# A hybrid block and a two-layer block on one core: the second block's weight halves written by transfers

## What is computed

```
h = concat(meta_tokens, x)                         # 528 x 1024
h = h + diff_attention(rms_norm(h), w_qkv) @ w_o   # 24 + 8 weight tiles
h = h + conv_ffn(rms_norm(h), w_up, w_down)        # 44 + 24
h = h + dsa_attention(rms_norm(h), w_in) @ w_o     # 31 + 8
h = h + conv_ffn(rms_norm(h), w_up, w_down)        # 44 + 24
h = rms_norm(h)
```

## Time and profile before

| | |
|---|---|
| median of 3 runs | 1819.41 us (1817.99 to 1821.04) |
| profiled execution, span from first to last instruction | 1818.3 us (no other time is given for it) |
| TensorE busy | 95% of the span, 14497 matmuls |
| VectorE, ScalarE, GpSimd busy | 65%, 35%, 6% |
| DMA | 160.57 MB, 88 GB/s on average |
| first block | up to about 395 us |
| run A, first attention, run B | 407 to 562, 562 to 649, 649 to 1297 us |
| second attention, run C | 1297 to 1384, 1384 to 1818 us |

### The profile page before, as it was taken

The page is one execution under the profiler, slowest core; times in us unless marked ns, Lnnn a source line. Parts: engine busy times, 40 slices in busy tenths (PEclk is TensorE's granted clock), DMA queues, the critical chain, the costliest instruction groups (busy, mean ns, idle before and its releaser), DMA issues.

```text
span 1818.3 us, 33711 instructions
## 1 busy us (share of the span) xinstructions
PE 1730.0 (95%) x14497; PEld 1558.3 (86%) x14497; DVE 1175.1 (65%) x2059; ACT 632.4 (35%) x1094; POOL 113.7 (6%) x71
## 2 busy tenths in 40 slices
PE   7999989978998889999999999999899999999997
PEld 3777779768996589999999999799668999999886
DVE  5237695447556876887774336698885677777334
ACT  3254442242114653222222222322485322222222
POOL 0001012000000000000000003234211000000000
PEclk9999969989999999999999999999899999999999
DMA  7521400032431013322222323334101232223332
GB/s 306 168 81 57 176 2 5 13 105 69 138 110 47 1 36 104 95 89 89 91 93 94 105 94 99 96 113 133 59 2 36 91 96 93 90 89 92 102 105 70
DMA packets 52565, 160.57 MB, mean 88 GB/s; under 512 B 8400, under 2 KB 11472, under 8 KB 52288
## 3 DMA queue, kind: packets, MB, share of 16 engines
q1 hardware_dynamic: 48544, 152.76, 26.1%
q10 hardware_dynamic: 3872, 5.65, 1.2%
HBM read 146.32 MB, written 2.10 MB: 82 GB/s over the span
## 4 chain that ended last, share of the span: by engine, by line
PE 76%; DVE 9%; issue 1%; ACT 1%; ACTq 0%; DVEq 0%
PE banks L603 21%; PE banks L604 20%; PE banks L605 20%; PE banks L2072 3%; PE banks L656 1%; PE banks L669 1%; DVE stat L1376 1%; PE banks L689 1%; PE banks L1831 1%; PE banks L1833 1%; PE banks L1832 1%; PE banks L934 1%; PE banks L732 1%; DVE arena L1386 1%; DVE w_lo L1274 0%
## 5 line engine op out<-in xcount | busy, mean ns | idle before, releaser
L603 PE MATMUL banks<-hn_hi,w_hi 128*128 128x264 f32 (+1 forms) x2272 | 651.0, 287 | 18.5 <-DVE hn_lo L1281 11.7
L604 PE MATMUL banks<-hn_lo,w_hi 128*128 128x264 f32 (+1 forms) x2272 | 644.7, 284 | 0.0
L605 PE MATMUL banks<-hn_hi,w_lo 128*128 128x264 f32 (+1 forms) x2272 | 644.1, 283 | 0.0
L1014 ACT ACTIVATE w_hi<-raw 128x1024 fp32r<-128x1024 f32 x205 | 217.4, 1061 | 808.9 <-PE banks L605 799.9
L603 PEld LDWEIGHTS banks<-hn_hi,w_hi 128*128 128x128 f32 x2272 | 430.0, 189 | 30.7 <-issue 27.0
L604 PEld LDWEIGHTS banks<-hn_lo,w_hi 128*128 128x128 f32 x2272 | 431.1, 190 | 0.1
L605 PEld LDWEIGHTS banks<-hn_hi,w_lo 128*128 128x128 f32 x2272 | 428.7, 189 | 0.0
L1274 DVE TENSOR_TENSOR w_lo<-raw,w_hi 128x1024 fp32r<-128x1024 f32 x175 | 214.2, 1224 | 179.7 <-ACT w_hi L1014 179.7
L603 PE MATMUL banks<-a_hi,w_hi 128*128 128x264 f32 (+1 forms) x506 | 160.4, 317 | 1.6 <-DVE u_in L1550 0.8
L604 PE MATMUL banks<-a_lo,w_hi 128*128 128x264 f32 (+1 forms) x506 | 160.7, 318 | 0.0
L605 PE MATMUL banks<-a_hi,w_lo 128*128 128x264 f32 (+1 forms) x506 | 160.6, 317 | 0.0
(11 more groups left out here) (431 smaller groups left out, 2679.3 us busy)
## 6 DMA issues: line engine op xcount, KB each, us to landing
raw<-in_weights SPq DMA_DIRECT2D x207, 512.0 KB, 3.5
ring<-in_weights SPq DMA_DIRECT2D x50, 512.0 KB, 4.4
arena<-arena SPq DMA_DIRECT2D x80, 66.0 KB, 2.0
arena<-arena ACTq DMA_DIRECT2D x64, 66.0 KB, 2.5
arena<-in_gate_w SPq DMA_DIRECT2D x8, 512.0 KB, 3.5
h<-in_xT SPq DMA_DIRECT2D x2, 1024.0 KB, 6.4
arena<-in_alibi SPq DMA_DIRECT2D x1, 1024.0 KB, 7.8
out_t<-h SPq DMA_DIRECT2D x2, 512.0 KB, 2.9
```

Of the source, the lines that this page charges most:

```text
L603: mm(o, w[0][:, j, :], x[0][:, k, lo:hi], start=first, stop=False)
L604: mm(o, w[0][:, j, :], x[1][:, k, lo:hi], start=False, stop=False)
L605: ins_ = mm(o, w[1][:, j, :], x[0][:, k, lo:hi], start=False, stop=last)
L1014: nc.scalar.activation(split_at(n)[0], raw[:, j % RAW, :], ACT.Copy).then_inc(S["w_hi_done"], 1)
```

## The change

Buffers: `raw` is gone; its room goes to `w_hi` and `w_lo`, which now have four tiles each (`W_RING`); the special places of two slots are gone too. All 207 slots are treated alike:

1. GpSimd issues a transfer of the slot from HBM into `w_hi` whose type is fp32r, so that the transfer rounds (`high_load`, semaphore `hi_loaded`).
2. ScalarE writes the negative of it into `w_lo`: `w_lo = -w_hi` (in `weight_high`, counted by `w_negated`).
3. GpSimd issues a second transfer of the same slot from HBM that adds to `w_lo`: `w_lo = w_lo + raw` (`low_sum`, semaphore `lo_summed`).
4. TensorE waits for `lo_summed`.

The 175 subtractions of VectorE and the 31 of GpSimd (with the last slot's, 207 in all) and SP's 207 loads are gone; 414 transfers issued from GpSimd take their place. ScalarE has as many instructions as before, with other sources and targets. `ahead(n)` now prepares slot n + 3. Some semaphores of the first block are shared where two of them could be one; that changes no instruction there.

The core of the diff:

```diff
@@ tensor_block2: slot(n)
-            pe.wait_ge(*split_of(n))
+            r, count = w_turn(n)
+            pe.wait_ge(lo_summed[r], count)
@@ pool_block2
-        def weight_rest(n):
-
-            pool.wait_ge(S["w_hi_done"], n - S_SPLIT + 1)
-            hi, lo = split_at(n)
-            g.tensor_tensor(lo, raw[:, (n - S_DA) % RAW, :], hi.bitcast(F32), ALU.subtract).then_inc(S["w_split_p"], 1)
+        def high_load(n):
+
+            if n >= N_SLOTS:
+                return
+            if n >= S_DA + W_RING:
+                pool.wait_ge(S["slot_used"], n - W_RING + 1)
+            g.dma_start(split_at(n)[0], ins["weights"][n]).then_inc(hi_loaded[w_turn(n)[0]], 16)
+
+        def low_sum(n):
+
+            if n >= N_SLOTS:
+                return
+            pool.wait_ge(S["w_negated"], n - S_DA + 1)
+            g.dma_start(split_at(n)[1], ins["weights"][n], accum_op=ALU.add).then_inc(lo_summed[w_turn(n)[0]], 16)
@@ pool_block2, the list
-        weight_rest(POOL_SLOTS[0])
+        pool.wait_ge(S["hn_ready"], 3 * KT)
+        for n in range(S_DA, S_DA + W_RING):
+            high_load(n)
+        for n in range(S_DA, S_DA + W_RING - 1):
+            low_sum(n)
         pool.wait_ge(S["norm_var"], 3)
         g.memset(da_qlast, 0.0).then_inc(S["zeroed"], 1)
-        pool.wait_ge(S["norm_var"], 5)
-        g.memset(qlast, 0.0).then_inc(S["zeroed"], 1)
-        for n in POOL_SLOTS[1:]:
-            weight_rest(n)
-        output_rests(8)
+        for n in range(S_DA, N_SLOTS):
+            if n == S_DSA + 6:
+                pool.wait_ge(S["norm_var"], 5)
+                g.memset(qlast, 0.0).then_inc(S["zeroed"], 1)
+            if n == S_DSAO:
+                output_rests(8)
+            low_sum(n + W_RING - 1)
+            high_load(n + W_RING)
@@ weight_high
-        act.wait_ge(S["slot_used"], S_DA if n == S_DA + 2 else S_DOWN1 if n == N_SLOTS - 1 else max(S_DA, n - SPLIT + 1))
-        j = n - S_DA
-        act.wait_ge(raw_loaded[j % RAW], 16 * (j // RAW + 1))
-        nc.scalar.activation(split_at(n)[0], raw[:, j % RAW, :], ACT.Copy).then_inc(S["w_hi_done"], 1)
+        r, count = w_turn(n)
+        act.wait_ge(hi_loaded[r], count)
+        if n < S_DA + W_RING:
+            act.wait_ge(S["slot_used"], S_DA)
+        nc.scalar.activation(split_at(n)[1], split_at(n)[0].bitcast(F32), ACT.Copy, scale=-1.0).then_inc(S["w_negated"], 1)
@@ act_block2: ahead(n)
-            weight_high(act, n + SPLIT)
+            weight_high(act, n + W_RING - 1)
@@ act_block2: the first projection
         for i in range(8):
-            if i:
-                ahead(S_DA + 2 * i)
+            ahead(S_DA + 2 * i)
             if i:
                 scatter(i - 1, (i - 1) % 4, to_plain_q if i <= 4 else to_k)
             ahead(S_DA + 2 * i + 1)
@@ the program of SP
-        sp.wait_ge(S["hn_ready"], 3 * KT)
-        for r in range(RAW):
-            sp.dma_start(raw[:, r, :], ins["weights"][S_DA + r]).then_inc(raw_loaded[r], 16)
-        for j in range(RAW, N_SLOTS - S_DA):
-            sp.wait_ge(*split_of(S_DA + j - RAW))
-            sp.dma_start(raw[:, j % RAW, :], ins["weights"][S_DA + j]).then_inc(raw_loaded[j % RAW], 16)
-            if S_DA + j in SCATTER_AFTER:
-                dsa_scatter(SCATTER_AFTER[S_DA + j])
+        for i in range(8, 18):
+            dsa_scatter(i)
```

More of the change, by code:

```diff
@@ L364, in build @@
     w_loaded = [sem(f"w_loaded{r}") for r in range(RING)]
-    raw_loaded = [sem(f"raw_loaded{r}") for r in range(RAW)]
+    hi_loaded = [sem(f"hi_loaded{r}") for r in range(W_RING)]
+    lo_summed = [sem(f"lo_summed{r}") for r in range(W_RING)]
     names = """once_dve once_pe once_act r_sums r_pointwise r_inputs r_norm_pe r_norm_dve r_norm_act slot_used params_in x_in consts_in meta_in out_stored dve_step act_step
@@ L552, in hn_base, with w_turn @@
         return KT * (v + 1)
-    POOL_SLOTS = (S_DA + 2, *range(S_DSA + 3, S_DSAO + 2))
     def split_of(n):
-        if n in POOL_SLOTS:
-            return S["w_split_p"], POOL_SLOTS.index(n) + 1
-        return S["w_split_d"], n - S_SPLIT + 1 - sum(m < n for m in POOL_SLOTS)
+        return S["w_split_d"], n - S_SPLIT + 1
+    def w_turn(n):
+        return (n - S_DA) % W_RING, 16 * ((n - S_DA) // W_RING + 1)
     def split_at(n):
[L563 to L567, removed]
+        r = w_turn(n)[0]
+        return w_hi[:, r, :], w_lo[:, r, :]
     END = (slice(META, META + T1 // 2), slice(META + T1 // 2, T2))
@@ L1219, in act_block2 @@
         ahead(S_DSA)
+        act.wait_ge(S["slot_used"], S_DSA + 1)
         A(halves(prob1(0)), pair(0), ACT.Square).then_inc(S["once_act"], 1)
@@ L1298, in norm_scale @@
                 V.tensor_scalar(r, psum[:, 6, 0:T1], 1.0 / D, EPS, ALU.mult, ALU.add).then_inc(S["norm_var"], 1)
-            if between is not None:
-                weight_low(between)
             ve.wait_ge(S["norm_std"], v + 1)
@@ L1313, in vector_block2, with rope @@
         cos2, sin2 = halves(cosT), halves(sinT)
-        def rope(i, s0, g, lows=True):
-            if lows and g:
-                weight_low(s0 + g + 2)
+        def rope(i, s0, g):
             ve.wait_ge(S["slot_used"], s0 + g + 2)
@@ L1326, in rope @@
             V.tensor_tensor(halves(rope_t(i, 3)), b, cos2, ALU.mult).then_inc(S["rope_read"], 1)
-            if lows and g:
-                weight_low(s0 + g + 3)
             ve.wait_ge(S["rope_read"], i + 1)
@@ L1519, in residual @@
             for g in range(groups):
-                for part in range(parts):
-                    n = s0 + parts * g + part
-                    if part < parts - 1:
-                        weight_low(n + 2)
-                ve.wait_ge(S["slot_used"], n + 1)
+                ve.wait_ge(S["slot_used"], s0 + parts * (g + 1))
                 x = h[:, g, tokens(v)]
@@ L1632, in vector_block2 @@
         for i in range(2):
-            rope(8 + i, S_DSA, G_QI + 2 * i, lows=False)
+            rope(8 + i, S_DSA, G_QI + 2 * i)
         def index_sums(u):
@@ L1670, in vector_block2 @@
                 i = 10 + (g - 9) // 2
-                rope(i, S_DSA, g - 2, lows=False)
+                rope(i, S_DSA, g - 2)
                 if i == 16:
@@ L1783, in _ @@
                 sp.dma_start(gate_w, ins["gate_w"][j]).then_inc(S["gate_in"], 16)
-        SCATTER_AFTER = {S_DSA + 10 + 2 * (i - 8): i for i in range(8, 18)}
         def dsa_scatter(i):
@@ L2485, in _ @@
         A(y1(N_OUT - 1), bank(OUT_BANKS[N_OUT - 1]), ACT.Copy)
-        for n in range(S_DA, S_DA + SPLIT + 1):
+        for n in range(S_DA, S_DA + W_RING - 1):
             weight_high(act, n)
```

62 lines of the change are left out of this document (20 added, 42 removed).

## The result

The changed kernel takes 2347.56 us (median of 4 runs, 2345.44 to 2352.77), against 1818.7 us for the kernel before beside it (1817.37 to 1821.04): a ratio of 1.2907, with a 95% interval of 1.2885 to 1.2929. It is 529 us slower. The forecast was 2130 us with a range of 1818 to 2500, and 0.86 for slower: sign and range held, the size was 218 us short.

A forecast was written before the change was run, and what follows sets the result against it. GpSimd's serial pass was to bound the changed kernel: 1.0 + 4.2 + 1.0 + 1.26 = 7.5 us a slot. Runs A, B, C added 26, 148, 137, together 311 us on 1818.3, giving 2130 us; range 1818 to 2500.

The forecast's parts named there:

- The mechanism: GpSimd's list runs each slot's rounding transfer, ScalarE's negative and the adding transfer's issue in series, 7.5 us a slot.
- the third: Step of GpSimd's pass: the rounding transfer queues behind the adding one issued before it; taken as 1.0 us.
- The upper bound of 2.4: Queueing delay of the rounding transfer, in us, if the adding transfer reads its target too and takes double.
- C: Time of one serial pass of GpSimd's list per slot: forecast 7.5 us, bounds 4.7 and 10.1.
- the second step: Step of GpSimd's pass: rounding transfer from issue to landing, 4.2 us, from SP's 3.5 plus 0.7 for longer issue.
- their way past the loads: SP's moves of queries and keys no longer stand behind loads: worth nothing, since TensorE waits for weights anyway.
- The 4.6 us stall: TensorE's wait for VectorE at the end of run B, where selection rounds finish late; claimed to go whatever happens.
- Fits into the slot time: Rival: GpSimd's pass stays under about 5.2 us, leaving only the root's delay, 1821 us; chance 0.08.
- Faster through VectorE: Rival: in the second projection VectorE, relieved, keeps ahead of TensorE and stalls go, 1815 us; chance 0.06.
- The adding transfer as the slow part: Rival: it holds DMA engines 5 us or more, or issues take over 2 us; 2632 us; chance 0.16.
- a spacing above 9 us: Sign in ScalarE's negatives that the adding transfer's price is wrong; 7.5 us apart was expected.
- Descriptors held up by VectorE: Rival: VectorE's fast SBUF instructions block GpSimd's descriptor writing, lengthening passes in up stages; no chance of its own.

The follow-up runs named there:

- the swap: Changed kernel with GpSimd's two issues exchanged, the next slots' rounding transfer ahead of the adding transfer: 1822.35 us, ratio 1.0012 to the kernel before.
- the run with swap and root: Changed kernel with GpSimd's two issues exchanged and ScalarE's norm_root(2) moved ahead of its second negative: 1817.61 us, ratio 0.9994 to the kernel before.
- The best version: Changed kernel with GpSimd's issues exchanged, norm_root(2) ahead of the second negative, and VectorE's selection rounds spread anew: 1812.94 us, ratio 0.9959 to the kernel before.

## Why the prediction was right, and where it fell short

**The mechanism** stood: one pass of GpSimd's list is serial, TensorE idles for a transfer before each slot (1.95 us on average over 152 times; 1.7 forecast), the pace is much the same in up and down stages, and the ring's depth does not matter between three and four. The forecast's own tests came out so: GpSimd waits for the negative and hardly for `slot_used`, and the root L1051 starts at 435.17 us (434 forecast). That last hit owes something to luck: the memset starts 1.15 us later in this run (427.07 for 425.92), and of the steps behind it the issue was shorter and the landing longer than forecast. The forecast's "about 7.5 us" for TensorE's restart is 7.9 by its own times (433.8 less 425.9); it came 8.9 us later, 1.2 of them the later start. That a lower clock only fills the gaps held too: the 171 us of longer matmuls did not set the pace, the pass did.

**The pass, term by term:**

| term | forecast | measured |
|---|---|---|
| issue of the adding transfer | 1.0 | 0.54 (the instruction lasts 0.86, and the next starts inside it) |
| rounding transfer to landing, by itself | 4.2 | 4.3 (when it goes first; 4.1 for the one at 1720.10 us, issued 3.9 us behind an adding one) |
| its queueing behind the adding one | 1.0 | 2.0 (6.3 less 4.3) |
| negative and hand-overs | 1.26 | 1.34 |
| pass | 7.5 | 8.2 |

The step that was mis-sized is the third, "I take 1.0 us": it measured 2.0. Behind a plain transfer the same landing is 4.5 us, 0.2 over the 4.3, so nearly all of the queueing is the sum's. The upper bound of 2.4 was named for the case that an adding transfer takes double, and it takes 1.5 to 1.9 times; I chose near the lower end. In the sum the miss was partly hidden, because the issue was put at 1.0 us and takes 0.54. The two together make 0.5 us, the other terms 0.2, and the pass comes out 0.7 us longer: 135 us at 193 passes.

The Trainium skill, Collectives: The Full Stack, The bandwidth ceiling, was weighed at this step. The estimate by its two source reads was C at 8.9 and a total of 2400 us, 52 us over the measured one; my choice is 218 us under it. The Trainium skill, DMA: Bandwidth & Descriptors, Specifications puts the first byte of a GpSimd-issued DMA at about 1 us, and the estimate by it was 3.9 us in place of 4.2 for the second step; at a measured 4.3 it was not the one that mattered.

**Where the rest went.** The three stretches of passes, read from the starts of the adding transfers:

| | passes | from, to (us) | mean | over 7.5, in us |
|---|---|---|---|---|
| run A | 19 | 435.56, 607.66 | 9.06 | 29.6 |
| run B | 103 | 727.77, 1607.22 | 8.54 | 107.0 |
| run C | 71 | 1725.59, 2315.59 | 8.31 | 57.5 |

The 194 us are most of the 214 by which the span's growth (525.3 us) passed the forecast's 311; 135 of them are the 0.7 us above. Near 40 more lie in run A and in the 31 passes of the second projection (1327.36 to 1607.22 us), whose means are 9.1 and 9.0 us against 8.3 elsewhere: there the moves of queries and keys share the DMA engines. I had put their way past the loads at nothing. For TensorE itself they are no matter (their landing went from 2.0 to 4.0 us on SP's queue and from 2.5 to 5.3 on ScalarE's), but the passes beside them are longer. The timeline of ScalarE in run A shows one of each kind:

```profile
461.68 1.06 ACT L1023 ACTIVATE w_lo<-w_hi 128x1024 fp32r<-128x1024 f32 x1 [7.23 <-DMA w_hi<-in_weights]
461.68 5.94 ACTq L1068 DMA_DIRECT2D arena<-arena  x8
471.75 1.06 ACT L1023 ACTIVATE w_lo<-w_hi 128x1024 fp32r<-128x1024 f32 x1 [9.01 <-DMA w_hi<-in_weights]
479.84 1.06 ACT L1023 ACTIVATE w_lo<-w_hi 128x1024 fp32r<-128x1024 f32 x1 [7.03 <-DMA w_hi<-in_weights]
```

With eight moves issued the pass takes 10.07 us, without them 8.09. Over run A the eight passes that have moves beside the rounding transfer take 10.2 us with a landing of 8.3, the eleven others 8.2 with 6.3. No run left the moves out, so this is read from passes of one run and not from an experiment. What is left of the 194, near 20 us, is spread over single passes with a later landing or issue.

The other 20 us lie outside the passes: the first one starts 1.8 us later than forecast (435.56 for 433.8), the way from run A's last pass to run B's first is 6.6 us longer (120.1 for 113.5), the way from run B's last to run C's first 10.3 (118.4 for 108.1), and the end takes 1.6 more (28.0 for 26.4). Of the 10.3 some 4 lie at the end of run B. At that end a wait stands that I had not foreseen, of TensorE in 1560 to 1660 us:

```profile
PE banks L631 <- ACT arena L1074: 18.9, 6, 7.4
```

ScalarE's copies of the values stand in its list behind negatives, and so behind a transfer. Here the pass would have held TensorE anyway.

**The 4.6 us stall** "should go whatever happens": in the changed kernel it went, where TensorE itself was late. With the swap it was back in full, 4.6 us. The reason was wrong: what cleared it, in both kernels, was another spread of the selection rounds, and taking the subtractions away did not.

**The rivals.** *Fits into the slot time*: it doesn't in this order, and with the order swapped the time is nearly the one worked out (1822.35 us for 1821), though not for its reason: the passes overlap, they don't get under 5.2 us. *Faster through VectorE*: its condition, a pass under 5 us, is not met; but its reading of the rotary sums was right. By form from 1090 to 1300 us, in the run with swap and root, against 1176 ns in the earlier trace rows (the mean of ten; the other sum, L1331, took 918):

```profile
L1324 DVE TENSOR_TENSOR arena<-arena 128x528 f32<-128x528 f32 x10 | 7.1, 708 | 0.3
```

The best version's 1812.94 us is that rival's place, reached with another spread of the rounds. *The adding transfer as the slow part*: it is slow, at 1.5 to 1.9 times a plain one, not three times, and no stretch averages over 9.5 us. The forecast's own sign for it, a spacing above 9 us, was met in run A and in the second projection, but by the passes beside moves. *Descriptors held up by VectorE*: it would have made the up stages longer. They are, by 0.1 to 0.2 us (8.4 against 8.2 in run B, 8.3 against 8.2 in run C; 8.3 against 8.2 with three pairs). VectorE is busy for 41% of the time there in run B (155.26 of 380 us) and for 9% in the down stage (15.86 of 180). No run took VectorE's work away, so the cause stays open; over the up stages' 88 slots it is worth under 20 us.

## What to carry to other kernels

When an engine issues transfers in a fixed list, write down what each entry waits for and what is queued behind it: a ring's depth buys nothing if the list waits on a hand-back for a pair right after it has issued that pair's first transfer. Issue what is only waiting for space first, and what waits for another engine after it; and put the transfer on the critical chain ahead of the bulky one, an adding one above all; in this kernel that was worth most of the gain (464 of 525 us). When work is moved off an engine that had room, expect nothing until the freed room is given to something that TensorE waits for.

## What the runs showed of the hardware

- A sum on the way into SBUF costs DMA time, and little of GpSimd's: 2.9 to 3.1 us of each DMA engine for 512 KB (estimates from the engines' shares, above) against 1.6 to 1.9 us. GpSimd's instruction for the plain second transfer lasts 0.53 us and for the adding one 0.86, and the next one starts 0.52 to 0.54 us after its start in either case.
- What stands ahead of a 512 KB rounding transfer in GpSimd's queue sets its landing: 6.3 us behind an adding transfer, 4.5 behind a plain one, 4.3 when it goes first. Rounding on the way cost nothing that can be seen (SP's plain load beside the same adding transfer took 4.4).
- DMA engines at 88 to 93% busy and 183 to 201 GB/s left TensorE at full clock and nearly without gaps: busy for 386.2 us of 387 from 703 to 1090 us and 354.2 of 356 from 1435 to 1791 us, in the run with swap and root.
- VectorE's sum of two SBUF tiles took 1176 ns on average where GpSimd subtracted in the same stretch, and 708 ns once it did not. The kernel before itself has the same line (L1330) at 702 ns in run A (430 to 600 us), where GpSimd does not subtract, so the other engine's instructions cost it some 40% of the time. The Trainium skill, SBUF — State Buffer, SBUF: two separate sides, says that a VectorE instruction with two SBUF inputs and a GpSimd instruction that reads SBUF exclude each other; these numbers agree.
- Small transfers pay for company: the 66 KB moves on SP's queue landed in 2.0 us before and in 4.0 with two weight transfers of 512 KB in each pass of 8 us (3.0 to 4.8 in the other runs with two weight transfers a slot).
